# S5 state space with states at every fourth token and matmuls with the last inputs; pooling means as matmuls with constant matrices

## What is computed

```python
def s5_mixer(u, lam_re, lam_im, log_dt, b_re, b_im, c_re, c_im, d_skip, w_glu):
    ...
    bu_re = jnp.einsum('bsgh,gph->sbgp', u32, bb_re)
    bu_im = jnp.einsum('bsgh,gph->sbgp', u32, bb_im)
    _, _, st_re, st_im = lax.associative_scan(_complex_linear_combine, (a_re, a_im, bu_re, bu_im), axis=0)
    y = (jnp.einsum('sbgp,ghp->bsgh', st_re, c_re.astype(F32))
         - jnp.einsum('sbgp,ghp->bsgh', st_im, c_im.astype(F32))
         + d_skip.astype(F32) * u32)
    y = jax.nn.gelu(y.reshape(bsz, s, D_A))
    out = y * jax.nn.sigmoid(y @ w_glu.astype(F32))

def pool_mixer(v, pool_w, pool_scale):
    ...
    for gi, w in enumerate(POOL_WINDOWS):
        ...
        means.append((c - lagged) / count)
    pooled = jnp.stack(means, axis=2) - v32
    mixed = jnp.einsum('bsgc,gcd->bsgd', pooled, pool_w.astype(F32))
```

## Time and profile before

| | |
|---|---|
| median of 3 runs | 1468.88 us (1468.85 to 1471.36) |
| the profiled execution's own time | 1467.95 us |
| its span | 1466.0 us |
| PE busy | 1324.5 us, 90% |
| DVE, ACT, POOL busy | 663.7 us (45%), 469.3 us (32%), 230.2 us (16%) |
| chain that ended last | PE 77%, DVE 12%, ACT 3%, DMA 3%, POOL 3%, issue 2% |
| granted TensorE clock, mean | 0.956 |

### The profile page before, as it was taken

One profiled execution on the slowest core, in us unless ns is written; L12 is line 12 of the kernel. 1 busy time (PEld: TensorE's weight loads), 2 busy tenths in 40 slices (PEclk: granted clock), 3 DMA queues, 4 the chain that ended last, 5 costly groups with the idle time before them and its releaser, 6 DMA issues.

```text
span 1466.0 us, 17831 instructions
## 1 busy us (share of the span) xinstructions
PE 1324.5 (90%) x7520; PEld 943.1 (64%) x7520; DVE 663.7 (45%) x872; ACT 469.3 (32%) x640; POOL 230.2 (16%) x235
## 2 busy tenths in 40 slices
PE   7999999978999999576899999995896989999994
PEld 6999979856999998334775444433785775444441
DVE  6654567554676555985551111116445362111113
ACT  5544346453434443212231011013476231011011
POOL 0000001300999201573000000000022100000000
PEclk9999999988999999878999999997998999999998
DMA  8545445503355543101568999996422257999994
GB/s 362 196 174 193 179 144 181 193 30 122 141 183 181 193 153 149 57 1 43 187 234 338 420 421 422 421 421 248 173 76 76 99 224 274 417 421 421 421 421 169
DMA packets 47316, 336.45 MB, mean 229 GB/s; under 512 B 5248, under 2 KB 5248, under 8 KB 7296
## 3 DMA queue, kind: packets, MB, share of 16 engines
q1 hardware_dynamic: 45936, 330.53, 57.7%
q10 hardware_dynamic: 1296, 4.72, 0.9%
HBM read 334.18 MB, written 1.05 MB: 229 GB/s over the span
## 4 chain that ended last, share of the span: by engine, by line
PE 77%; DVE 12%; ACT 3%; DMA 3%; POOL 3%; issue 2%; SPq 0%; ACTq 0%; DVEq 0%
PE pb L177 76%; DVE halves L291 3%; DMA ring<-in_moe_w 1%; ACT halves L283 1%; DMA XN<-in_ln_b 1%; DMA ring<-in_ffn_w 1%; DVE SM L1347 1%; DVE Xs L1358 1%; POOL p L1315 1%; DVE p L1250 1%; POOL p L1313 1%; PE pb L1784 0%; POOL p L1312 0%; DVE p L1513 0%; DVE Xs L385 0%
## 5 line engine op out<-in xcount | busy, mean ns | idle before, releaser
L291 DVE TENSOR_TENSOR halves<-ring,halves 128x2048 fp32r<-128x2048 f32 (+1 forms) x122 | 287.9, 2370 | 185.9 <-ACT halves L283 185.6
L177 PE MATMUL pb<-XTh,halves 128*128 128x256 f32 x1920 | 353.3, 285 | 13.6 <-DVE p L1527 7.5
L177 PEld LDWEIGHTS pb<-XTh,halves 128*128 128x128 f32 x1920 | 303.8, 193 | 16.3 <-DVE p L1527 8.1
L177 PE MATMUL pb<-XTl,halves 128*128 128x256 f32 x960 | 273.0, 284 | 0.0
L283 ACT CAST halves<-ring 128x2048 fp32r<-128x2048 f32 (+1 forms) x122 | 227.5, 1873 | 114.8 <-PE pb L177 111.0
L177 PE MATMUL pb<-ring,gather 128*64 128x512 f32 x1024 | 233.3, 597 | 3.2 <-DVE gather L1913 1.7
L177 PEld LDWEIGHTS pb<-XTl,halves 128*128 128x128 f32 x960 | 185.5, 193 | 0.9
L177 PE MATMUL pb<-halves,XTh 128*128 128x512 f32 x480 | 151.4, 397 | 10.4 <-DVE XTl L367 3.6
L177 PEld LDWEIGHTS pb<-ring,gather 128*64 128x64 f32 x1024 | 71.1, 137 | 133.9 <-issue 129.7
L177 PE MATMUL pb<-ring,slots_ht 128*64 128x512 f32 x512 | 118.5, 605 | 3.2 <-DMA ring<-in_moe_w 1.3
L1909 DVE TENSOR_TENSOR slots_h<-slots_silu,pb 128x256 f32<-128x256 f32 x32 | 13.5, 421 | 229.2 <-ACT slots_silu L1874 229.2
(11 more groups left out here) (306 smaller groups left out, 1378.6 us busy)
## 6 DMA issues: line engine op xcount, KB each, us to landing
ring<-in_moe_w SPq DMA_DIRECT2D x192, 1024.0 KB, 12.8
ring<-in_ffn_w SPq DMA_DIRECT2D x66, 1024.0 KB, 4.8
ring<-in_w_tok SPq DMA_DIRECT2D x10, 1024.0 KB, 4.8
ring<-in_ple_gate SPq DMA_DIRECT2D x8, 1024.0 KB, 4.8
ring<-in_w_out SPq DMA_DIRECT2D x4, 1024.0 KB, 4.8
ring<-in_ab_in SPq DMA_DIRECT2D x4, 1024.0 KB, 4.7
ring<-in_ab_out SPq DMA_DIRECT2D x4, 1024.0 KB, 4.7
ring<-in_sb_v SPq DMA_DIRECT2D x4, 1024.0 KB, 23.4
```

Of the source, the lines that this page charges most:

```text
L177: return e.matmul(out, l, r, start=start, stop=stop, **kw)
L291: e.tensor_tensor(l, raw_of(n), h.bitcast(F32), ALU.subtract).then_inc(*low.mark(n))
```

## The change

The states are kept at tokens 4m + 3 only, 64 positions. Per block of states the input of position m is the sum over n of L^n B u(4m + 3 - n), n = 0 to 3, made on PE with four tables `BK` (B times powers of L). The four blocks that share a slice a (q = 0 to 3) stand side by side in one bank, 4 x 64 real and 4 x 64 imaginary columns, and one `unit(a)` of DVE turns, scans and turns back all four at once; the scan's factor is the fourth power of the decay, with a zero where a new q begins. POOL makes the imaginary part of the states. The output of token 4m + n is C L^(n+1) s(4m - 1) (`pe_outputs`) plus the last inputs straight through a 128 x 128 matrix `KL` for each lag 0 to 3 and each q, which holds C L^l B on its 32 x 32 blocks and, at lag 0, the skip D (`pe_direct`). `KL` comes from 32 matmuls (`pe_recent`) and copies by ACT and DVE. L itself, laid out for `BK`, is computed on 128 x 512 elements in asides of the second FFN (`act_lam`, `dve_lam`). Three inputs are new: `s5k` (0.79 MB), `s5b` and `windows` (0.52 MB each).

The pooled means less v are twelve fp32 matmuls with constant matrices (`pe_windows`). For that v is projected with tokens on the partitions, by `pe_tok` and 48 matmuls of 512 columns in place of 96 of 256.

```diff
+        plan_all("ab_u", a["ab_u"])
+        plan_all("ab_v", a["ab_v"])
...
+        def act_lam(e, step):
+            if step == 0:
+                e.wait_ge(l_k, 16)
+                e.activation(lk_dt, lk_dt, ACT.Exp).then_inc(*k_dt.mark())
+            else:
+                e.wait_ge(*k_turns.at())
+                e.activation(lk_re, lk_re, ACT.Exp)
+                e.activation(lk_t, lk_im, ACT.Sin)
+                e.activation(lk_dt, lk_im, ACT.Sin, scale=0.5).then_inc(*k_sin.mark())
...
+        def pe_recent(e):
+            e.wait_ge(l_sb, 16)
+            e.wait_ge(*tables_done.at())
+            for q in range(4):
+                for x in range(2):
+                    for a_ in range(4):
+                        r, j = slice(32 * a_, 32 * a_ + 32), 4 * q + a_
+                        i = mm(e, banks[2][r, q * 128:q * 128 + 128], b_lanes[:, x, j, :], CW[:, :, x, j, :], x == 0, x == 1,
+                               skip_group_check=True)
+            i.then_inc(*recent_done.mark())
...
+        def pe_inputs(e):
+            e.wait_ge(*in_kept.at(1))
+            for q in range(4):
+                for x in range(2):
+                    for n in range(4):
+                        for a_ in range(4):
+                            r, o_ = slice(32 * a_, 32 * a_ + 32), x * 256 + q * 64
+                            i = mm(e, banks[4 + a_][:, o_:o_ + 64], BK[3 - n][x][r, q, :], u4[r, q, :, n], n == 0, n == 3)
+            i.then_inc(*x_done.mark())
+
+        def pe_direct(e, q):
+            y4 = y_bank(q).rearrange("p (m i) -> p m i", i=4)
+            if q == 0:
+                e.wait_ge(*recent_dve.at("skip"))
+            e.wait_ge(*rotated.at(q))
+            for l in range(4):
+                mm(e, y4[:, :, l:4], KL[:, l, q, :], u4[:, q, :, 0:4 - l], l == 0, False, skip_group_check=True)
+
+        def pe_outputs(e, pair):
+            for a_ in pair:
+                e.wait_ge(*state_re.at(a_))
+                e.wait_ge(*state_im.at(a_))
+            for q in range(4):
+                y4 = y_bank(q).rearrange("p (m i) -> p m i", i=4)
+                for n in range(4):
+                    for x in range(2):
+                        for a_ in pair:
+                            r, j = slice(32 * a_, 32 * a_ + 32), 4 * q + a_
+                            i = mm(e, y4[r, 1:64, n], CW[:, n, x, j, :], ST[:, a_, x, q, 0:63], False, n == 3 and x == 1,
+                                   skip_group_check=True)
+                if pair[1] == 3:
+                    i.then_inc(*y_done.mark(q))
...
+        def pe_windows(e):
+            e.wait_ge(*v_kept.at(1))
+            e.wait_ge(*recent_act.at(1))
+            e.wait_ge(*recent_dve.at(1))
+            e.wait_ge(l_pm, 16)
+            for g in range(4):
+                P, o_, d = banks[2 + g // 2], g % 2 * 256, slice(g * 128, g * 128 + 128)
+                mm(e, P[:, o_:o_ + 128], VT3[:, 0, d], PM[:, g, 0, :], True, True)
+                mm(e, P[:, o_ + 128:o_ + 256], VT3[:, 1, d], PM[:, g, 1, :], True, False, skip_group_check=True)
+                i = mm(e, P[:, o_ + 128:o_ + 144], VT3[:, 0, d], con("pcross", 16 * g, 16), False, True, skip_group_check=True)
+                if g % 2:
+                    i.then_inc(*windowed.mark(g // 2))
...
+            pe_recent(e)
+            pe_inputs(e)
+            pe_tok(e, "ab_v", 0, 1)
+            for q in range(4):
+                pe_direct(e, q)
+            pe_outputs(e, (0, 1))
+            pe_windows(e)
+            pe_outputs(e, (2, 3))
+            pe_pool_mix(e)
             blk, W = weights(e, "w_glu", k=4)
             e.wait_ge(*y_low.at(3))
-            e.wait_ge(*bu_cos.at(15))
             for mp in range(2):
-                P = banks[1 + 3 * mp]
+                P = banks[4 + 2 * mp]
                 for c in range(2):
                     m = 2 * mp + c
                     for k in range(4):
                         i = mm3(e, P[:, c * 256:c * 256 + 256], both(W, lambda x: x[:, k, m * 128:m * 128 + 128]),
                                 both(ygs, lambda x: x[:, k, :]), k == 0, k == 3)
                 i.then_inc(*(glu_half.mark() if mp == 0 else used.mark(blk)))
+            e.wait_ge(*pool_low.at(3))
...
+            e.dma_start(PM, a["windows"].rearrange("p (g c t) -> p g c t", g=4, c=2)).then_inc(l_pm, 16)
+            act_split(e, c, index["ab_v", 1] + SPLIT)
+            for gp in range(2):
+                e.wait_ge(*windowed.at(gp))
+                e.copy(yh[:, gp * 512:gp * 512 + 512], banks[2 + gp][:, :]).then_inc(*win_high.mark(gp))
+            for g in range(4):
+                if g % 2 == 0:
+                    e.wait_ge(*(used.at(index["pool_w"]) if g else pool_mixed.at()))
+                e.activation(XT3[0][:, 4 + g, :], banks[g // 2][:, g % 2 * 256:g % 2 * 256 + 256], ACT.Copy,
+                             scale=par("ps", g, 1)).then_inc(*pool_high.mark(g))
+            e.wait_ge(*rotated.at("all"))
+            for q in range(4):
+                e.wait_ge(*y_done.at(q))
+                e.activation(yg3[:, q, :], y_bank(q), ACT.Gelu_apprx_tanh).then_inc(*y_gelu.mark(q))
+                e.wait_ge(*y_gelu.now())
+                e.copy(ygs[0][:, q, :], yg3[:, q, :]).then_inc(*y_high.mark(q))
+            act_split(e, c, index["pool_w"] + SPLIT)
...
+            def unit(a_):
+                X, z = banks[4 + a_], ZZ[a_ % 2]
+                turn = CS5[:, a_, :, :, :].rearrange("p c q m -> p (c q m)")
+                r = R4[:, a_, :, :].rearrange("p q m -> p (q m)")
+                if a_ >= 2:
+                    e.wait_ge(*state_im.at(a_ - 2))
+                e.tensor_tensor(RA, X[:, :], turn, ALU.mult)
+                e.tensor_tensor(RB[:, 0:256], X[:, 0:256], turn[:, 256:512], ALU.mult)
+                e.tensor_tensor(RB[:, 256:512], X[:, 256:512], turn[:, 0:256], ALU.mult).then_inc(*rotated.mark(a_))
+                e.wait_ge(*rotated.now())
+                e.tensor_tensor(RW[:, 0:256], RA[:, 0:256], RA[:, 256:512], ALU.add)
+                then(e.tensor_tensor(RW[:, 256:512], RB[:, 256:512], RB[:, 0:256], ALU.subtract))
+                e.tensor_tensor_scan(z[:, 0:256], r, RW[:, 0:256], 0.0, ALU.mult, ALU.add)
+                e.tensor_tensor_scan(z[:, 256:512], r, RW[:, 256:512], 0.0, ALU.mult, ALU.add).then_inc(*decayed.mark(a_))
+                e.wait_ge(*decayed.now())
+                then(e.tensor_tensor(RP, z, turn, ALU.mult))
+                s = ST[:, a_, 0, :, :].rearrange("p q m -> p (q m)")
+                e.tensor_tensor(s, RP[:, 0:256], RP[:, 256:512], ALU.subtract).then_inc(*state_re.mark(a_))
+
+            dve_split(e, c, index["ab_u", 1] + 2)
+            e.wait_ge(*recent_done.at())
+            e.wait_ge(*recent_zero.at())
+            for a_ in (2, 3):
+                r = slice(32 * a_, 32 * a_ + 32)
+                i = e.tensor_copy(KL[r, :, :, r], banks[2][r, :].rearrange("p (q l h) -> p l q h", q=4, l=4))
+            i.then_inc(*recent_dve.mark(1))
+            e.wait_ge(*recent_dve.now())
+            e.wait_ge(*recent_act.at(1))
+            for q in range(4):
+                i = e.scalar_tensor_tensor(KL[:, 0, q, :], ident, par("sd", q, 1), KL[:, 0, q, :], ALU.mult, ALU.add)
+            i.then_inc(*recent_dve.mark("skip"))
+            e.wait_ge(*x_done.at())
+            unit(0)
+            dve_split(e, c, index["ab_v", 0] + 2)
+            unit(1)
+            dve_split(e, c, index["ab_v", 1] + 2)
+            unit(2)
+            unit(3)
+            e.wait_ge(*state_re.now())
+            e.wait_ge(*state_im.at(3))
+            e.tensor_copy(RW[:, 0:1], RW[:, 0:1]).then_inc(*rotated.mark("all"))
+            for gp in range(2):
...
+            dve_split(e, c, index["w_glu"])
+            for g in range(4):
+                P = banks[g // 2]
+                e.wait_ge(*pool_high.at(g | 1))
+                e.scalar_tensor_tensor(XT3[1][:, 4 + g, :], P[:, g % 2 * 256:g % 2 * 256 + 256], par("ps", g, 1),
+                                       XT3[0][:, 4 + g, :].bitcast(F32), ALU.mult, ALU.subtract).then_inc(*pool_low.mark(g))
+            for q in range(4):
+                e.wait_ge(*y_high.at(q))
+                e.tensor_tensor(ygs[1][:, q, :], yg3[:, q, :], ygs[0][:, q, :].bitcast(F32), ALU.subtract).then_inc(*y_low.mark(q))
+            dve_split(e, c, index["pool_w"] + SPLIT)
...
+            e.memset(KL, 0.0).then_inc(*recent_zero.mark())
+            for a_ in range(4):
+                z = ZZ[a_ % 2]
+                e.wait_ge(*decayed.at(a_))
+                if a_:
+                    e.wait_ge(*state_im.at(a_ - 1))
+                e.tensor_tensor(RQ[:, 0:256], z[:, 0:256], CS5[:, a_, 1, :, :], ALU.mult)
+                e.tensor_tensor(RQ[:, 256:512], z[:, 256:512], CS5[:, a_, 0, :, :], ALU.mult).then_inc(*c.chain.mark())
+                e.wait_ge(*c.chain.now())
+                e.tensor_tensor(ST[:, a_, 1, :, :], RQ[:, 0:256], RQ[:, 256:512], ALU.add).then_inc(*state_im.mark(a_))
...
```

(5 more changed lines are left out.)

386 lines of the change are left out of this document (166 added, 220 removed).

## The result

The changed kernel took 1414.07 us in the median of four runs (1412.02 to 1417.24), the kernel before 1469.17 (1468.85 to 1471.36, four runs). The ratio is 0.962, with an interval from 0.960 to 0.965: 55.1 us less, where the forecast had 42.5 and a range of 1411 to 1446. The profiled run of the changed kernel took 1412.02 us, its span is 1410.2; the spans differ by 55.8.

The account below looks back on a forecast made before the run. The S5 stage, 119.0 us with PE mostly waiting on DVE and POOL, was taken as the bound. The new terms sum to 72.5 us, 76.5 with the clock: gain 42.5, forecast 1426.4 us, range 1411 to 1446.

Parts of the forecast that it names:

- p: Price in us of one pair on PE, a weight load and a pass of a small matmul; taken as 0.05.
- the rival of four-way overlap: Four PE tiles overlap wholly: p 0.027, stage 63 us, gain 56, 1413 us; chance 0.13.
- (b): Small matmuls, PE's new work on the path: 576 pairs at 0.05; recent and inputs 16.0 us, outputs 2 x 6.4.
- (c): DVE and POOL on the path: four units replace sixteen cycles, 21.2 us from the end of `pe_inputs`.
- (d): Behind the units: `pe_direct(3)` 1.2, windows 2.9, `pe_pool_mix` 1.45, ACT wait 6.3, w_glu 7.4, to out-projection 3.2 us.
- (e): PE's half clock after idle: 3 us at `pe_direct(3)` and the outputs' start, 1 in w_glu, together 4.
- ACT's tail: Wait ahead of w_glu for pooling halves, a table load, gelus and casts on ACT, and DVE's low half: 6.3 us.
- the price of a pair: Cost of a small matmul's weight load plus pass on PE: 0.05 us taken, ends 0.027 and 0.107.
- the slowest rival: Small matmuls neither overlap nor lift the clock: p 0.214, stage 171 us, 1521 us; chance 0.03.
- 47.7 + 576 p: Forecast length in us of the new S5 stage for any p; breaks even at p = 0.124.
- Step (a): New tables made in the second FFN by ACT, DVE and POOL, with three new loads: cost 0.
- 75 us of cover: Slack for POOL's tables in the second FFN: ended at 493 us, first needed at 569.

Follow-up runs that it names:

- contiguous: Changed kernel with inputs reading 64 neighbouring columns of u and outputs writing 63 neighbouring columns of y, instead of every fourth; 1416.7 us, one run.
- gelu_early: Changed kernel with ACT's four gelus and high halves ahead of pool_high, and DVE's low halves of y ahead of pool_low; 1412.3 us, one run.
- changed_again: The changed kernel once more, without an edit, on the same chip as the run with the edits combined; median 1415.66 us, five runs.

## Why the prediction was right, and where it was off

It got the direction, the mechanism and the path right, and its range held. But the case that it held likeliest (p from 0.035 to 0.075, gain 28 to 51) did not come: the gain was 55.1, 12.6 more than forecast, p was 0.029, and the time lies beside the 1413 of the rival of four-way overlap, for whose sake the range had been drawn down to 1411. Term by term, from the end of the u projection:

| step | forecast | measured | difference |
|---|---|---|---|
| (b) `pe_recent` and `pe_inputs` | 16.0 | 13.35 | -2.65 |
| (c) units, up to direct(3) | 21.2 | 20.2 | -1.0 |
| (d), (e) direct(3), outputs(0, 1), 3 of clock | 10.6 | 6.6 | -4.0 |
| (d) windows | 2.9 | 2.8 | -0.1 |
| (b) outputs(2, 3) | 6.4 | 3.6 | -2.8 |
| (d) `pe_pool_mix` and ACT's tail | 7.75 | 7.5 | -0.3 |
| (d), (e) w_glu, 1 of clock | 8.4 | 7.8 | -0.6 |
| (d) to the out-projection | 3.2 | 2.8 | -0.4 |
| sum | 76.5 | 64.65 | -11.8 |

**The term that failed is the price of a pair.** The text took 0.05 us, "the row nearest in shape", from four weight loads of 64 columns. It cost 0.029 at the full clock in all three shapes, just what the rival of four-way overlap gave (0.027), which had a chance of 0.13. The evidence for it stood in the text: two row tiles took 1.14 us where one took 1.13. The four loads show how close loads can start, but not what a load and its pass cost in a row: in PE's row of the kernel before from the same start, 16 passes of 512 columns take 3.65 us, 0.228 each.

```profile
769.52 3.65 PE L177 MATMUL pb<-ring,gather 128*64 128x512 f32 x16
```

Without overlap a pair costs 0.116, close to the 0.107 that bounded it from above, and 0.213 at half the clock, the 0.214 of the slowest rival. At p = 0.029 the text's own formula, 47.7 + 576 p, gives 64.4, and 64.65 were measured. That it is so near is luck: in the inputs some 4 us of gap and clock came on top, and the other terms together were 3.8 too long. The Trainium skill ("TensorEngine Tiling (Array Packing)", Instruction Overhead) counts about 60 cycles for each matmul; the estimate of 0.05 for a pair that was worked out from it does not agree with the measured 0.029. The Trainium skill ("TensorEngine Tiling (Array Packing)", Theoretical Speedup) gives up to four times for a dimension of 32, and the trace agrees, 0.116 to 0.029.

**The clock was near in sum and wrong in place.** Forecast were 4 us, 3 at direct(3) and the outputs, 1 at w_glu. At the first it cost some 1.5 us (1.91 for direct(3) where the same matmuls took 1.49 at the full clock in contiguous, 4.80 for outputs where 3.71 are enough). W_glu took 7.76 us, 0.3 over the 7.44 of before; gelu_early's 5.7 shows that the 7.44 held a spell at half the clock already. But 3.0 us came where none were forecast, in the middle of the inputs: the last 126 records took 6.7 us where 126 x 0.029 is 3.65. The pause in front of them cost 0.9 more from one record's start to the next. The sentence that 256 records in a row leave no gaps, and that PE has the full clock where it is dense, was wrong: they left a gap, and dense with 32-row matmuls they lost the clock. At p = 0.05 for the inputs the error was hidden, since the mean over both halves was 11.4 / 256 = 0.044.

**The rest held.** The units took 5.06, 4.97 and 4.95 us with splits of 1.14 and 2.75 between, where the text had 5.1 each, 3.4 for the splits and 0.9 for a slowing beside POOL. PE waited for ACT's tail of pooling halves, table load and gelus. The out-projection followed w_glu by 2.84 us; the splits queued there cost nothing yet, and cost 3.9 in gelu_early, where the wait ahead of w_glu was shorter and w_glu faster. One reading of the stage before was off: in its chain DVE's L1250 stands sixteen times, but POOL's pair L1315, L1316 only ten times; in the other blocks DVE's weight splits, the pooling's sums, the skip or ACT stand there. No term of the sum rests on it.

**Step (a), no cost in the second FFN, held.** This row of the chain, PE's run through that FFN, has the same length in the kernel before (first) and in the changed one.

```profile
371.01 188.51 PE pb L177 x1320
```

```profile
372.53 188.52 PE pb L177 x1320
```

Its length was 188.50 to 188.52 in all profiles. POOL's tables ended at 516 us, not at 493: most of their operations of 512 columns took 1.7 to 2.6 us in the mean, not 1.57, and the one product with a constant (`tensor_scalar`) 5.8. Of 75 us of cover 53 were left.

**The totals.** The second FFN begins 1.5 us later in the changed kernel, and between 371.4 and 376.7 in the profiles of the experiments. In the changed kernel 0.25 us of it come from the first weights; the rest arises in the mixing stage ahead, where 8 matmuls took 2.79 us for 1.56 before. Behind the stage, rows of the same matmuls differ both ways, 9.91 to 8.52, 8.16 to 6.78, 19.92 to 21.57. In each the longer one holds more time at half the clock. All such differences sum to 2.9 us in favour of the changed kernel in this profile; runs of one and the same kernel lie up to 6.6 us apart (changed_again), those of the kernel before on that chip up to 8.3. Whether the later start has a part that belongs to the change stays open, since only one profile of the kernel before was taken.
